# Early expert matrices, a moved table operand and a late modulation in a mixture-of-experts layer on one core

## The reference

```
sh_m, sc_m, g_m, sh_f, sc_f, g_f = _modulations(c, ada_w, ada_b)
...
x = x + g_m * y                                   # residual of the mixer
xn = _rmsnorm(x, norm_ffn_g) * (1.0 + sc_f) + sh_f
x = x + g_f * _moe(xn)                            # g_f: the feed-forward modulation
...
scores = sigmoid(x @ router_w); _, idx = top_k(scores + bias, 8)
hid    = silu(x @ exp_w_gate[e]) * (x @ exp_w_up[e])
routed = sum over e of (hid * gate[e]) @ exp_w_down[e]
shared = (silu(x @ shared_w_gate) * (x @ shared_w_up)) @ shared_w_down
```

## Time and profile before

| | |
|---|---|
| median of 3 runs | 798.7 us (798.02 to 800.08) |
| the profiled execution | 799.33 us, span 797.6 us |
| TensorE busy, matmuls | 700.1 us, 88% of the span |
| DMA | 279.15 MB, 350 GB/s on average |
| queue of SyncE (q1) | 252.35 MB |
| queue of GpSimd (q0) | 26.07 MB |
| mean granted TensorE clock | 0.976 |

### The profile page before, as it was taken

How to read it: one execution, slowest core, us unless ns; L and a number is a source line. 1 busy time by engine, 2 the same in 40 slices (tenths; PEclk the granted TensorE clock), 3 DMA queues, 4 the chain that set the end, 5 groups by cost and what they waited for, 6 DMA issues and landing times.

```text
span 797.6 us, 15126 instructions
## 1 busy us (share of the span) xinstructions
PE 700.1 (88%) x5157; PEld 408.9 (51%) x5158; DVE 328.7 (41%) x615; ACT 225.2 (28%) x389; POOL 301.3 (38%) x317
## 2 busy tenths in 40 slices
PE   4999899999999999999999989998789977997930
PEld 3765556446555446545565656454355543543510
DVE  3262278477344552344323332434323433243217
ACT  5130612023223331233223222323222332232212
POOL 0050112021306544545544562636435454455130
PEclk9999999999999999999999999999999999999975
DMA  8976998829689999999999999999999999999943
GB/s 335 416 219 231 350 345 300 346 79 386 223 329 381 393 411 370 340 382 391 395 381 395 387 396 404 387 407 399 408 414 401 400 400 410 398 402 402 359 99 130
DMA packets 60206, 279.15 MB, mean 350 GB/s; under 512 B 18997, under 2 KB 20289, under 8 KB 32764
## 3 DMA queue, kind: packets, MB, share of 16 engines
q1 hardware_dynamic: 36520, 252.35, 78.3%
q0 software_dynamic: 23424, 26.07, 13.7%
q10 hardware_dynamic: 212, 0.08, 0.0%
HBM read 272.54 MB, written 26.30 MB: 375 GB/s over the span
## 4 chain that ended last, share of the span: by engine, by line
PE 61%; DMA 28%; DVE 5%; issue 3%; SPq 1%; ACT 1%; POOL 0%; POOLq 0%; DVEq 0%; ACTq 0%
PE bank L1140 25%; DMA gu<-in_exp_w_up 24%; PE bank L1176 10%; PE bank L854 4%; PE bank L872 4%; PE bank L1003 4%; PE bank L1118 2%; DMA gu<-in_ada_rest 2%; PE bank L842 2%; PE bank L913 1%; PE bank L875 1%; PE bank L1232 1%; DMA gu<-in_mix_w 1%; PE bank L1157 1%; PE bank L1087 1%
## 5 line engine op out<-in xcount | busy, mean ns | idle before, releaser
L1140 PE MATMUL bank<-gu,et 128*64 128x256 f32 x2496 | 283.3, 380 | 32.0 <-DMA gu<-in_exp_w_up 26.8
L1140 PEld LDWEIGHTS bank<-gu,et 128*64 128x64 f32 x2496 | 188.9, 137 | 144.0 <-issue 73.4
L544 POOL DMA_INDIRECT acc_rows<-et,idx x64 | 104.6, 1634 | 242.4 <-DVE et L1667 141.4
L1176 PE MATMUL bank<-dn,et 128*64 128x512 f32 x632 | 150.6, 601 | 12.4 <-issue 10.0
L1660 DVE COPY et<-bank 128x256 f32<-128x256 f32 x64 | 27.2, 424 | 255.7 <-PE bank L1157 234.8
L737 ACT ACTIVATE et<-bank 64x512 f32<-64x512 f32 x64 | 37.8, 591 | 261.9 <-PE bank L1140 237.3
L1176 PEld LDWEIGHTS bank<-dn,et 128*64 128x64 f32 x632 | 42.7, 136 | 78.0 <-issue 76.9
L747 ACT ACTIVATE et<-bank,mb 128x512 f32<-128x512 f32 x64 | 44.0, 687 | 120.3 <-PE bank L1176 98.2
L1667 DVE TENSOR_SCALAR et<-bank,mb 128x512 f32<-128x512 f32 x64 | 48.1, 751 | 68.3 <-PE bank L1176 54.4
L1653 DVE TENSOR_TENSOR et<-et 64x512 f32<-64x512 f32 x64 | 67.9, 1061 | 0.5 <-ACT et L738 0.4
L554 POOL DMA_DIRECT2D small<-halfc x49 | 56.3, 1148 | 0.0
(11 more groups left out here) (289 smaller groups left out, 622.1 us busy)
## 6 DMA issues: line engine op xcount, KB each, us to landing
dn<-in_exp_w_down SPq DMA_DIRECT2D x64, 1024.0 KB
gu<-in_exp_w_gate SPq DMA_DIRECT2D x63, 1024.0 KB
gu<-in_exp_w_up SPq DMA_DIRECT2D x63, 1024.0 KB
gu<-in_ada_rest SPq DMA_DIRECT2D x8, 2048.0 KB, 11.0
gu<-in_mix_w SPq DMA_DIRECT2D x4, 2048.0 KB, 12.9
gu<-in_lru_in_w SPq DMA_DIRECT2D x4, 1024.0 KB, 15.0
gu<-in_sgu_in_w SPq DMA_DIRECT2D x2, 2048.0 KB, 13.8
gu<-in_out_w SPq DMA_DIRECT2D x2, 2048.0 KB, 11.5
```

The lines of the kernel that those rows point to most:

```text
L544: pool.indirect_dma_start(acc_rows[u % 2], bass.IndirectOffsetOnAxis(ap=idx[:, u, 0:1], axis=0), yo[:, u % 2, 0, :], None, bounds_check=2 ...
L1140: mm = pe.matmul(bank[u % 2][64 * c:64 * c + 64, b * FE:(b + 1) * FE], xt[:, b, k % 4, k // 4, :], w[c][:, k * FE:(k + 1) * FE], start=(k ...
L1176: mm = pe.matmul(bank[5 + b][64 * c:64 * c + 64, :], hT[:, b, j, :], dn[:, dslot(u), j * D + c * HALF:j * D + (c + 1) * HALF], start=(j == ...
```

## The change

Down matrices 0 to 3 are issued ahead of the pairs of experts 1 and 2. The table's operand moves from place 3 of `dn` to the place of `yo`, the shared expert's sigmoid rows move from there to the place of `up`. Expert 5's gate matrix goes to `gmod` after the mixer's residual, expert 4's up matrix to `late` once the counts are made, both ahead of expert 3's pair. Since `gmod` is taken, g_f is read by GpSimd behind scatter 5, when expert 5's product is done, and `SHARED_AT` goes from 5 to 10. TensorE's program has one more `body` outside its loop.

```diff
-SHARED_AT = 5
+SHARED_AT = 10
...
+        gmodf = gmod[:, :, :].rearrange("p a n -> p (a n)")
...
-        sgs = et[:, 5120:5376]
+        sgs = up[:, 0:FE]
...
         def mv(r, h):
-            home = xTf if r else dnf[:, 3 * 2 * D:4 * 2 * D]
+            home = xTf if r else yo_f
...
-                sync.dma_start(guf[sl][:, 0:KT * FE], eg[e]).then_inc(ld_gu[sl], 16)
+                if not (isinstance(g, int) and g == SLOTS + 1):
+                    sync.dma_start(guf[sl][:, 0:KT * FE], eg[e]).then_inc(ld_gu[sl], 16)
...
+            sync.wait_ge(s["ya_done"], CT)
+            sync.wait_ge(s["mix_free"], 1)
+            for u in range(SLOTS):
+                load_dn(0, 0, u)
             load_gu(0, 0, 1)
             load_gu(0, 0, 2)
-            sync.wait_ge(s["ya_done"], CT)
-            sync.wait_ge(s["mix_free"], 1)
-            for u in range(3):
-                load_dn(0, 0, u)
+            sync.wait_ge(ld_shared_gu, 16)
+            sync.wait_ge(s["x2_done"], 3)
+            sync.wait_ge(ld_gu[gslot(SLOTS + 1, SLOTS + 1)], 32)
+            sync.dma_start(gmodf, eg[SLOTS + 1]).then_inc(ld_gu[gslot(SLOTS + 1, SLOTS + 1)], 16)
+            sync.wait_ge(s["acc_zeroed"], 32)
+            sync.wait_ge(s["counted"], 1)
+            sync.dma_start(late[:, :], eu[SLOTS]).then_inc(ld_shared_gu, 16)
             load_gu(0, 0, 3)
-            sync.wait_ge(s["acc_zeroed"], 32)
             sync.dma_start(xTf[:, 0:KT * FE], eg[SLOTS]).then_inc(ld_shared_gu, 16)
-            sync.dma_start(late[:, :], eu[SLOTS]).then_inc(ld_shared_gu, 16)
             load_gu(0, 0, SLOTS + 1)
             load_gu(0, 0, SLOTS + 2)
             sync.wait_ge(s["tb_mm"], TOP)
-            load_dn(0, 0, 3)
...
             pool.wait_ge(s["gf_wrote"], 64)
-            get_mods(5, gmod[:, 0, :], gmod[0:64, 1, :], "gf_in")
...
+                    if first and r == 0 and u == SLOTS + 2:
+                        pool.wait_ge(s["gu_done"], SLOTS + 2)
+                        get_mods(5, gmod[:, 0, :], gmod[0:64, 1, :], "gf_in")
...
                 w = (xTf, late) if special else (guf[sl], guf[sl][:, KT * FE:2 * KT * FE])
+                if isinstance(e, int) and e == SLOTS + 1:
+                    w = (gmodf, w[1])
...
-                with pe.Fori(3, NE // V - 1) as i:
+                body(r, 3)
+                with pe.Fori(4, NE // V - 1) as i:
```

More of the change, by code:

```diff
@@ L157, in build @@
         hT = part(256).rearrange("p (s j n) -> p s j n", s=2, j=2)
-        yo = part(2048).rearrange("p (a s n) -> p a s n", a=2, s=2)
+        yo_f = part(2048)
+        yo = yo_f.rearrange("p (a s n) -> p a s n", a=2, s=2)
         shT = et[:, o[0]:o[0] + 256].rearrange("p (j n) -> p j n", j=2)
-        sgs = et[:, 5120:5376]
+        sgs = up[:, 0:FE]
         up_s = xnf[0:64, 2 * D:2 * D + FE]
```

## The result

The changed kernel is slower: 805.44 us, the median of 6 executions (803.83 to 806.13), against 800.13 for the kernel before in the same comparison (6 executions, 798.02 to 800.96). The ratio is 1.0072 [1.0052, 1.0092], or +5.8 us (4.2 to 7.4). The prediction was 797.2 with a range to 801.5; it was wrong, in sign too. The cause is the mechanism of the third rival, larger than it was priced: the two copies of g_f (the feed-forward modulation) hold up gather 10 in GpSimd's queue.

The account below looks back on a forecast made before the run. Loads wait for TensorE until about 230 us, both run without pause to about 447, then the load stream sets the end. From 798.7: -2.6 + 2.0 + 1.2 - 2.1 = -1.5, so 797.2 us, range 793.4 to 801.5.

Parts of the forecast that it names:

- third rival: GpSimd's queue: g_f copies delay gather 10, TensorE waits 5 us, scatter 6 may add 3; 801.8 us, chance 0.16.
- first and third term: Load stream: down 3 loaded early, -2.6 us; new dry gaps near 237 and 241 us, +1.2 us.
- second: Saturated stage, about 274 us: g_f's 0.79 MB, now issued behind scatter 5, costs +2.0 us of load stream.
- fourth: Load gap at 316 to 319.75 us closes because expert 11's product ends 9.2 us earlier: -2.1 us.
- the sum, without any queueing: Whole kernel: the four terms together give -1.5 us, so 797.2 us; chance 0.48.
- margin of 5.1: TensorE at expert 13: its product ends 5.1 us earlier than before; the third rival decides only if more is lost.
- near 309.4: TensorE: expert 11's product ends 9.2 us earlier, after the shared down products move to experts 10 to 15.

Follow-up runs that it names:

- experiment 5: The changed kernel with g_f read early, expert 5's gate matrix in its old place and SHARED_AT back at 5: 799.3 us, 0.9999 of the kernel before.
- experiments 2 and 8: experiment 2, and the kernel before with SHARED_AT 10, the table's operand moved and only down 0 to 3 early: 794.66 us, 0.9944.
- experiment 1: The changed kernel with the two copies of g_f issued from ScalarE's queue, 5.4 us earlier: 796.62 us, 0.9981 of the kernel before.
- experiment 2: The changed kernel with g_f read early, ahead of the first gather, and expert 5's gate matrix in its old place: 795.44 us, 0.9949 of the kernel before.
- experiment 6: The kernel before with SHARED_AT = 10 and one more unrolled body, nothing else: 795.02 us, 0.9951.
- experiment 3: The kernel before with g_f read behind scatter 5, SHARED_AT = 10 and one more unrolled body: 805.9 us, 1.0077.
- experiment 4: The changed kernel with 60 turns of the identity on TensorE ahead of its wait for gather 10: 803.33 us, 1.0055 of the kernel before.
- Experiments 9 to 12: Changed kernel: 9 without samples' copy, 1.0004; 10 without prompt's, 1.0034; samples' copy from one row, 11 without prompt's, 0.9987, 12 with it, 1.0027.

## Why the prediction was wrong

| step of the prediction | forecast | measured |
|---|---|---|
| down 3 early and new gaps (first and third term) | -1.4 us | experiment 5: -0.1 (-1.9 to +1.8), spent again at 318; experiments 2 and 8 beside 6: about -0.2 and -0.6, not to be told from 0 or from -1.4 |
| bytes of g_f in the full stage (second) | +2.0 | experiment 1 against 2: 0.0032 x 800 = +2.6, uncertain by about 3, so not to be told from 0 or from 2.0 |
| gap at 318 closed (fourth) | -2.1 | experiment 6: -3.9 (-6.2 to -1.5) |
| the sum, without any queueing | -1.5 | experiment 1: -1.5 (-3.8 to +0.7) |
| gather 10 held in GpSimd's queue | a rival, chance 0.16 | changed kernel against experiment 1: +7.3, uncertain by about 3 |

The sum was right for a kernel in which the copies stand in nobody's way, in part by luck: as far as the runs tell, early down 3 gave nothing, and the closed gap gave more than its term (-0.2 + 2.6 - 3.9 = -1.5). The step that failed is the sentence that gives g_f a price, "0.79 / 400 GB/s = +2.0 us". It prices the copies by bytes in the load stream, and leaves what they hold up to a rival. Measured, the late copies cost 10.1 us (experiment 3 against 6, uncertain by about 4).

I had the place, the queue and the order right in that rival, and went wrong three times in its size and chance.

First, the landing. I took 14.3 us, the median of two copies, neither of which ran in the full stage (from 187 to 202 us, behind the later one's issue, the share was 0.88). Here it took 17.0. The clock times hide that, since this execution stands some 1.4 us earlier throughout (expert 6's matrices are issued at 227.83 in place of 229.20) and the copies followed scatter 5 after 1.6 us in place of 2.5: the second copy landed at 289.8 where I had 289.2. Gather 10's first half landed at 291.7, its second at 293.8, where I had 292 for both, while TensorE was due at 285.8 and not at 286.8. So the wait was 8.3 and not 5 us.

Second, the clock. I forecast a wait and not what TensorE does after it. The wait brings the 1.2 GHz level for 10 us, 2.7 us more (experiment 4). With both, expert 10 ends 11 us late against a margin of 5.1. Scatter 6, from which I expected 3 us, shows no wait of its own: VectorE and ScalarE wait for no DMA there. At expert 13 the changed kernel is 343.80 - 334.01 = 9.8 us behind experiment 2, and 11.3 when counted from the issue of expert 6's matrices (227.83 and 229.33), which is what it lost at expert 10.

Third, the argument against it: "before, the token rows' stores stood ahead in the same queue, which are absent here". I took the 14.3 us as a sign of what stood ahead of the copy. Experiments 9 to 12 show that the samples' copy is itself slow, 2.8 us of wait by the shape of its source, and that it slows the loads' packets. I had one number for both copies and read only the bytes out of it.

The rest of the path came as described. TensorE's products in experiment 2 signal at 309.43 and 334.01, where the prediction had "near 309.4" and 338.82 - 5.1 = 333.7. The stretch 226 to 231 stayed thin (0.39), and the down matrices went out at 147.30 into the empty hole (share 0.77 from 157 to 168). TensorE waited over 5 us for gather 10 and a gap opened between 319 and 345, both of which the prediction had named as what would make it wrong.

The gap at 318 seems to have been worth more than the share in its 3.75 us says. The kernel before, then experiment 6, from 316 to 345 us:

```profile
316.00:327.00 11.00, 10.90 (x83) 6.22 (x78) 2.99 (x5) 2.70 (x5) 1.65 (x1) 1.00 0.79 281
327.00:345.00 18.00, 17.76 (x136) 9.93 (x134) 6.30 (x10) 4.71 (x8) 10.35 (x9) 1.00 1.04 350
```
```profile
316.00:327.00 11.00, 11.00 (x72) 5.49 (x70) 4.73 (x8) 2.47 (x4) 5.21 (x5) 1.00 1.04 367
327.00:345.00 18.00, 17.58 (x119) 8.96 (x116) 6.77 (x13) 4.25 (x7) 6.21 (x7) 1.00 1.04 389
```

Experiment 6 moves 11 x 86 + 18 x 39 = 1650 KB more than the kernel before, 4.1 us at 400 GB/s, and experiment 2 (375 and 373 GB/s) 1450 KB, 3.6 us, against my 2.1. I had read only the stretch in which the share was low and a little of the ramp behind it. The full stage runs at 1.03 and not at 1.00 as well. The time of experiment 6, -3.9 us, leaves room for 2.1 too (-6.2 to -1.5).

Three versions beat the kernel before, by 0.5%: experiments 2, 6 and 8. The simplest is the kernel before with `SHARED_AT = 10` and one more unrolled body, 795.02 us. Four or five matrices loaded early add nothing measurable to it.

## What to carry to other kernels

A transfer put into a queue of gathers is priced by the gather behind it and not by its bytes: ask which consumer waits for the next entry, and take the landing time under the load of that stage. If it must go there, look for a queue whose next entries are not urgent; ScalarE's took the same 0.79 MB, issued 5.4 us earlier, for 7.3 us less. A wait on TensorE can also cost the products after it, at half the clock: 2.7 us behind a wait of 8.3 here.

## What the runs showed of the hardware

- With a copy of 256 KB from eight rows ahead of the gather, TensorE waited 5.1 us for it, with the same bytes from one row 2.3, and with 512 KB from one row over 128 partitions 3.0.
- While a copy over 64 partitions ran, the loads' packets took 409 ns on average, where they took 278 beside the copy over 128 partitions, and the core moved 300 GB/s in place of 426 at a DMA share of 1.06 and 1.03. Why is open; a busy share says nothing of the rate then, and GB/s has to be read beside it.
- After the waits of 8.3, 5.4, 5.1 and 2.3 us TensorE's first products ran at 1.2 GHz in part or in whole: 3.68, 3.68, 2.75 and 2.68 us for a down product of 1.94, with a granted clock of 0.50 in the 10 us after the longest. After the wait of 1.1 us in experiment 1 the clock stayed at 1.00 (286 to 300 us).
